# Two-layer hybrid step on one core: output halves weighted before the norm's factor is known, three-pass channel transform, two PSUM groups for the first mLSTM heads, three VectorE passes moved

## The chip, the cores and the metric

One core of one Trainium2 chip runs the whole program in one launch. The metric is device microseconds of one execution. Before the change it is 2081.56 us, the median of 3 runs (2080.41 to 2082.77). Engines are named as in the profile: PE (TensorE matmul), PEld (TensorE weight load), DVE (VectorE), ACT (ScalarE), POOL (GpSimd), SP (SyncE, which issues most DMAs).

## The reference, cut to what matters

1152 tokens (128 of context, 1024 latent) of width 1024 pass two layers. In both, `h = rms_norm(x, g_pre) * (1 + scale) + shift`, a mixer makes `y`, and

```python
x = x + gate * rms_norm(y, g_post)       # rms_norm(y, g) = y * rsqrt(mean(y*y) + EPS) * g
```

Layer 0 has two mixers side by side. The RG-LRU mixer (8 blocks of 128 channels) projects, convolves, gates and scans. The Fourier mixer (8 blocks of 128 channels) computes, for each block,

```python
fr = jnp.fft.fft2(xg, axes=(1, 3), norm='ortho').real        # over tokens and the block's 128 channels
yb = jnp.einsum('blgi,gij->blgj', fr, w_four) + b_four
y  = concat([ya * silu(za), yb * silu(zb)]) @ w_out
```

Layer 1 is a chunkwise mLSTM with 8 heads in both directions: for each head q, k, v, o, z are projected, input and forget gates of all heads come from 32 more columns (`log_sigmoid` of the forget gate, running sums and running maxima over tokens), and 9 chunks of 128 tokens are stepped through.

## The kernel before, in words

**Precision and tiling.** A weight matrix or activation that goes through a large product is split into a high part, rounded to a single-pass format (fp32r, written by ACT), and the rest (`raw - hi`, subtracted by DVE). A product is then three matmul passes: hi x hi, hi x rest, rest x hi. Projections are 8 slices of the contraction times 3 passes times 3 column groups of 384 tokens, 72 matmuls into one PSUM group of three banks (`project`, L126). `PS` holds two groups of three banks, `PX` two more banks. Some small products are single passes on plain fp32; the profile shows two records for each.

**Staging of weights.** `w_load` (SP), `w_split_hi` (ACT, L107) and `w_split_lo` (DVE, L111) bring every 128-column weight tile through two slots. A tile is loaded when its slot's rest has been taken, split high when the product that used the slot has ended, and PE waits for the rest (`w_lo`).

**Order.** Each engine runs a list written out by hand, stage by stage, and waits on semaphores; nothing is reordered at run time. The stages are setup, RG-LRU blocks, Fourier blocks, output product of layer 0 with the next layer's norm, mLSTM heads, output product of layer 1.

**Setup (L420-543).** x is normed, turned and modulated into `h` in 8 slices. ACT writes the even slices' modulated rows and all high parts (L164, L442), DVE the odd slices' modulated rows (L516) and the rests (`h_rows`, L521). DVE takes the rest of the first weight tile inside `h_rows(0)`, between the odd slice's rows and the first slice's rest. The first RG-LRU steps follow: DVE clears the padded input (L816), then computes a softplus (L551 on), and ACT waits for both.

**Fourier blocks (L902-1171).** In block i PE multiplies the channel DFT with `w_four` (L981), projects xb (L126, group 0), in blocks 2 to 5 also sums a part of the remaining modulation (L1011), does the token transform of block i-1 (L997, L1000), then turns xb of block i against the channel weights (`to_tokens`, L987: 9 token tiles, 128x128 against 128x256, 6 into group 0 and 3 into `PX`), and projects zb (L126, group 1). ACT copies xb out of PSUM (L1061) and the 256 channel-weight columns (L1058), both as fp32. On DVE, `outputs(i-1)` (L1137, L1138) waits for the token transform; its end (`y_ready`) lets PE start the zb projection.

**Output product (L1173-1497).** 18 half tiles of 128 tokens x 512 columns, first the left halves, then the right halves, into three banks in turn. When the right half of tile t is done, ACT sums its squares (L1357, written to the scratch `OUTB`) and takes the root (L1361); DVE inverts it (L1427), multiplies both halves by the inverse and the gain rows (L1429, L1431), and adds the residual to the right half (L1435), while POOL adds it to the left half (L1288). In layer 0, ACT then norms x again, PE turns it to channels (L1299), and DVE modulates it in PSUM (L1447) and takes the rest of `h` (L1452). At the end PE computes the gate columns and the first q tile by column groups (L144).

**mLSTM heads (L1551-2230).** `body(j, ...)` projects head j's 8 tiles ("jobs" 0 to 7: q, k, two v tiles, o, z, o, z; job n of head j is written (j, n) below) and steps head j-1's chunks between them. `body(0)` has only jobs 0 to 3. All jobs use PSUM group 0, and PE starts a job when the one before has been copied out by ACT (`pe.wait_ge(evacuated, before(j, n))`); group 1 and `PX` hold the head's chunk work. In `body(0)` DVE works through `forget_gates`: rows of 40 x 1152 elements through a logarithm (`log1p`: a reciprocal, then a series), sums and maxima, with the rests of weight tiles 2 to 5 (jobs (0,2), (0,3), (1,0), (1,1)) put between by a hook. ACT then takes four exponentials (L1944-1947), PE turns them to token order (`gates_to_tokens`, L1743, into group 1), DVE copies them out (`token_scalars`, L2021), PE turns k (L1762) and forms the scores (L1764), DVE weighs k (L2048), and then takes the rest of the next v tile.

## Time and profile before

| | |
|---|---|
| median of the runs | 2081.56 us |
| the profiled execution's own time | 2082.77 us |
| its span, first to last instruction | 2081.2 us, 28432 instructions |
| busy: PE, PEld | 2022.2 us (97%), 1891.3 us (91%) |
| busy: DVE, ACT, POOL | 1049.6 us (50%), 651.8 us (31%), 129.6 us (6%) |
| granted TensorE clock, mean | 0.994 of full speed |

Shares are of the span. The page's second part cuts the span into 40 slices; PE shows nine tenths or more in all but three of them, at the start, in the sixteenth slice (780 to 832 us) and at the end. A row of the trace names an engine, a line of the kernel, the operation, what is written and read, and, in square brackets, how long the engine stood idle just before and what ended that. "x72" is a count of instructions merged into one row.

### The profile page before, as it was taken

What the parts mean: (1) busy time and instruction counts of PE and PEld (TensorE: products, weight loads), DVE (VectorE), ACT (ScalarE), POOL (GpSimd) and SP (SyncE); (2) the same over time, 40 slices, a digit from 0 to 9 for tenths busy, and PEclk for the clock granted to TensorE, in tenths of its full rate; (3) what the DMA queues carried; (4) which work ended last, traced back from release to release, by engine and by line L of the source; (5) the groups of instructions that cost most, each with busy time, mean ns of one, the idle gap of its engine ahead of it and who ended that gap; (6) DMA issues with size and microseconds to landing.
All of it is one profiled execution on the core that took longest, in us unless ns stands there. A gap on an engine that the chain in (4) does not pass through costs nothing.

```text
span 2081.2 us, 28432 instructions
## 1 busy us (share of the span) xinstructions
PE 2022.2 (97%) x11770; PEld 1891.3 (91%) x11770; DVE 1049.6 (50%) x1632; ACT 651.8 (31%) x831; POOL 129.6 (6%) x117
## 2 busy tenths in 40 slices
PE   6999999999999998999999999999999999999998
PEld 5999999999988888989999999999999999998886
DVE  5778885535353574763434334343343433545344
ACT  6677773222234453121212112121121111214422
POOL 0032232000200010000000000000000000000001
PEclk9999999999999999999999999999999999999999
DMA  8221214442246443131221312213122121416554
GB/s 296 66 67 43 73 58 120 142 169 82 70 153 186 153 157 113 35 113 41 82 59 38 102 41 82 59 41 99 41 81 59 46 95 41 101 58 193 174 167 136
DMA packets 218344, 204.59 MB, mean 98 GB/s; under 512 B 13346, under 2 KB 187002, under 8 KB 218098
## 3 DMA queue, kind: packets, MB, share of 16 engines
q1 hardware_dynamic: 214194, 190.52, 30.3%
q0 software_dynamic: 3872, 12.35, 1.7%
q8 instruction: 87, 1.43, 0.3%
q14 instruction: 31, 0.25, 0.0%
q10 hardware_dynamic: 160, 0.05, 0.0%
HBM read 172.14 MB, written 30.59 MB: 97 GB/s over the span
## 4 chain that ended last, share of the span: by engine, by line
PE 80%; issue 8%; POOL 3%; DVE 3%; ACT 3%; DMA 2%; ACTq 0%; POOLq 0%; SPq 0%; DVEq 0%
PE psum_groups L126 37%; PE psum_groups L1207 18%; PE psum_groups L1823 10%; PE psum_groups L1804 3%; PE psum_extra L1795 3%; PE psum_groups L1806 2%; POOL tanh_then_state L635 2%; DMA w_raw<-in_w_in_e 1%; PE psum_groups L997 1%; POOL mixed_y L640 1%; PE psum_groups L144 1%; PE psum_groups L987 1%; PE psum_extra L1011 1%; PE psum_groups L1764 1%; PE psum_groups L1775 1%
## 5 line engine op out<-in xcount | busy, mean ns | idle before, releaser
L126 PE MATMUL psum_groups<-h_hi,w_hi 128*128 128x384 f32 x1896 | 449.5, 345 | 11.4 <-ACT q_t L1916 4.2
L126 PE MATMUL psum_groups<-h_lo,w_hi 128*128 128x384 f32 x1896 | 434.3, 337 | 0.0
L126 PE MATMUL psum_groups<-h_hi,w_lo 128*128 128x384 f32 x1896 | 434.1, 337 | 0.0
L126 PEld LDWEIGHTS psum_groups<-h_hi,w_hi 128*128 128x128 f32 x1896 | 339.1, 188 | 23.0 <-issue 12.6
L126 PEld LDWEIGHTS psum_groups<-h_lo,w_hi 128*128 128x128 f32 x1896 | 340.3, 188 | 0.0
L126 PEld LDWEIGHTS psum_groups<-h_hi,w_lo 128*128 128x128 f32 x1896 | 340.1, 188 | 0.0
L1207 PE MATMUL psum_groups<-w_out,y_tile_hi 128*128 128x512 f32 x1008 | 317.6, 394 | 0.0
L1207 PEld LDWEIGHTS psum_groups<-w_out,y_tile_hi 128*128 128x128 f32 x1008 | 189.6, 188 | 42.6
L2089 DVE SCALAR_TENSOR_TENSOR state<-state,head_decay,psum_extra 128x257 f32<-128x257 f32 x112 | 54.1, 483 | 287.6 <-PE psum_groups L1806 285.5
L1207 PE MATMUL psum_groups<-w_out,y_tile_lo 128*128 128x512 f32 x504 | 198.1, 393 | 0.0
L1823 PE MATMUL psum_groups<-w_hi,h_hi 128*128 128x256 f32 x576 | 165.1, 287 | 4.9 <-DVE w_lo L111 2.1
L111 DVE TENSOR_TENSOR w_lo<-w_raw,w_hi 128x1024 fp32r<-128x1024 f32 x97 | 133.8, 1379 | 68.9 <-ACT w_hi L107 60.9
L1823 PE MATMUL psum_groups<-w_lo,h_hi 128*128 128x256 f32 x576 | 163.1, 283 | 0.0
L1823 PE MATMUL psum_groups<-w_hi,h_lo 128*128 128x256 f32 x576 | 163.1, 283 | 0.0
L107 ACT ACTIVATE w_hi<-w_raw 128x1024 fp32r<-128x1024 f32 x97 | 102.5, 1056 | 70.6 <-PE psum_groups L1823 37.6
L1823 PEld LDWEIGHTS psum_groups<-w_hi,h_hi 128*128 128x128 f32 x576 | 109.3, 190 | 7.0 <-ACT v_rows L1920 3.2
L1207 PEld LDWEIGHTS psum_groups<-w_out,y_tile_lo 128*128 128x128 f32 x504 | 94.8, 188 | 20.8
L1823 PEld LDWEIGHTS psum_groups<-w_lo,h_hi 128*128 128x128 f32 x576 | 109.5, 190 | 0.0
L1823 PEld LDWEIGHTS psum_groups<-w_hi,h_lo 128*128 128x128 f32 x576 | 109.4, 190 | 0.0
L1288 POOL TENSOR_TENSOR x_rows_residual<-out_first_half,x_rows_residual 128x512 f32<-128x512 f32 x18 | 23.3, 1294 | 1356.8 <-DVE out_first_half L1429 1356.8
L273 DVE TENSOR_TENSOR y_tile_lo<-y_tile_raw,y_tile_hi 128x512 fp32r<-128x512 f32 x126 | 80.0, 684 | 35.7 <-ACT y_tile_hi L269 35.2
L1926 ACT ACTIVATE o_tanh<-psum_groups 128x1152 f32<-128x1152 f32 x16 | 18.1, 1132 | 252.6 <-PE psum_groups L126 252.6
(316 smaller groups left out, 2485.7 us busy)
## 6 DMA issues: line engine op xcount, KB each, us to landing
w_raw<-in_w_in_o SPq DMA_DIRECT2D x65, 512.0 KB, 5.2
y_tile_raw<-y_scratch SPq DMA_DIRECT2D x126, 256.0 KB, 3.0
w_raw<-in_w_in_e SPq DMA_DIRECT2D x32, 512.0 KB, 4.0
w_mod_rest<-in_w_mod SPq DMA_DIRECT2D x4, 4096.0 KB, 14.8
y_scratch<-mixed_y POOLq DMA_DIRECT2D x16, 576.0 KB, 3.5
decay_matrix<-gate_rows SPq DMA_DIRECT2D x8, 1152.0 KB, 7.4
q_carry<-gate_rows SPq DMA_DIRECT2D x8, 1152.0 KB, 6.4
y_scratch<-out_gate SPq DMA_DIRECT2D x8, 1152.0 KB, 5.2
```

Source lines behind the costliest of these rows:

```text
L107: act.activation(WHI[:, slot, :], WRAW[:, slot, :], ACT.Copy).then_inc(w_hi, 1)
L111: dve.tensor_tensor(WLO[:, slot, :], WRAW[:, slot, :], WHI[:, slot, :].bitcast(F32), ALU.subtract).then_inc(w_lo, 1)
L126: ins = pe.matmul(PS[:, group, j, 0:JW], w[:, slot, k * P:(k + 1) * P], h(k0 + k)[:, j * JW:(j + 1) * JW], start=start and k == 0 and m == ...
L273: eng.tensor_tensor(y_lo_at(l, n, c), y_raw_at(l, n, c), y_hi_at(l, n, c).bitcast(F32), ALU.subtract).then_inc(yo_lo, 1)
L635: pool.tensor_tensor(both, both, HT[:, 1, p0:p0 + t1 - t0], ALU.add).then_inc(summed, 1)
L1207: ins = pe.matmul(bank(n), y, w[part], start=k == 0 and m == 0, stop=k == 2 * KC - 1 and m == 2)
L1288: pool.tensor_tensor(XR[:, t % 2, 0:DH], out_half(t), XR[:, t % 2, 0:DH], ALU.add).then_inc(x_pool, 1)
L1795: ins = pe.matmul(KV[d][:, 0:DV1], KW[:, d, t * P:(t + 1) * P], V[q][:, t, :], start=True, stop=True)
L1804: ins = pe.matmul(NUM[d][:, 0:DV1], DM[q][:, d, cols], V[q][:, t, :], start=True, stop=s == 0)
L1806: ins = pe.matmul(NUM[d][:, 0:DV1], QW[:, d, cols], C[:, d, :], start=False, stop=True)
L1823: ins = pe.matmul(dst, h[:, k, t * P:(t + 1) * P], w[:, slot, cols], start=k == 0 and m == 0 and n % 2 == 0, stop=k == KC - 1 and m == 2, ...
L2089: ins = dve.scalar_tensor_tensor(C[:, d, :], C[:, d, :], DC[:, d, tiles[d]:tiles[d] + 1], KV[d][:, 0:DV1], ALU.mult, ALU.add)
```

## The change

It has five parts.

1. *Output halves.* DVE multiplies both halves by the gain rows as soon as they are there, the right one after the squares are summed, and then, with the inverse root, does `half * inverse + residual` for both halves. POOL's addition is gone. ACT writes its squares to a PSUM bank, not to `OUTB`.
2. *Channel transform.* In Fourier blocks 1 to 7 `to_tokens` is three single-pass matmuls a tile (27, not 9 fp32 products). ACT writes xb and the channel weights rounded; DVE takes both rests (`operands_rest`), 256 and 1152 columns from PSUM, ahead of `outputs(i-1)`. PE waits for them.
3. *First heads.* Jobs (0,1), (0,3) and (1,1) write PSUM group 1; jobs (0,1) to (1,1) wait for the job before the last. `gates_to_tokens` uses group 0 and waits for (1,0)'s copy, and after it PE waits for (1,1)'s.
4. *DVE passes moved.* The first weight tile's rest goes ahead of `h_rows(0)`; the clearing of the padded input goes into setup; in `forget_gates` the rest of tile (1,0) goes one instruction later in the series; in `body(1)` the rest of tile (1,2) goes from behind `weigh_k` to ahead of it.
5. The buffers get new names and places for it.

```diff
             modulation_vectors(0)
+            w_split_lo(dve, 0, 0)
             for k in range(HALF):
-                h_rows(k, (lambda: w_split_lo(dve, 0, 0)) if k == 0 else None)
+                h_rows(k)
             w_split_lo(dve, 0, 1)
+            dve.memset(XA[:], 0.0).then_inc(pads, 1)
             modulation_vectors(1)
...
+        ch.link(dve.scalar_tensor_tensor(E, E, 1.0, S, ALU.add, ALU.mult))
         if between:
-            between("summed")
-        ch.link(dve.scalar_tensor_tensor(E, E, 1.0, S, ALU.add, ALU.mult))
+            between("series_ready")
...
-            def to_tokens(first, last, bank, done):
+            def to_tokens(i, first, last, bank, done):
+                passes = ((XB, CW), (XBL, CW), (XB, CWL)) if i else ((XB0, CW0),)
                 for t in range(first, last):
-                    ins = pe.matmul(bank(t - first), XB[:, t * P:(t + 1) * P], CW[:].rearrange("p a n -> p (a n)"),
-                                    start=True, stop=True, skip_group_check=True)
+                    for m, (x, w) in enumerate(passes):
+                        ins = pe.matmul(bank(t - first), x[:, t * P:(t + 1) * P], w[:].rearrange("p a n -> p (a n)"),
+                                        start=m == 0, stop=m == len(passes) - 1, skip_group_check=True)
...
             def modulation(i, q):
-                pe.wait_ge(cw_out, i + 1)
+                pe.wait_ge(operands_lo, 2 * i - 1)
...
-                pe.wait_ge(xb_out, i + 1)
-                pe.wait_ge(cw_out, m * 2 + slot + 1)
+                if i:
+                    pe.wait_ge(operands_lo, 2 * i)
...
+            def operands_rest(i):
+                dve.wait_ge(cw_out, i + 1)
+                dve.tensor_tensor(CWL[:].rearrange("p a n -> p (a n)"), PX[:, 1, 256:512],
+                                  CW[:].rearrange("p a n -> p (a n)").bitcast(F32), ALU.subtract).then_inc(operands_lo, 1)
+                dve.wait_ge(xb_out, i + 1)
+                dve.tensor_tensor(by_bank(XBL[:]), PS[:, 0, :, 0:JW], by_bank(XB[:]).bitcast(F32), ALU.subtract
+                                  ).then_inc(operands_lo, 1)
...
                     w_split_lo(dve, i + KC, 1)
+                    operands_rest(i)
                     outputs(i - 1, isinstance(i, int) and i == 1)
...
-                pool.tensor_tensor(XR[:, t % 2, 0:DH], out_half(t), XR[:, t % 2, 0:DH], ALU.add).then_inc(x_pool, 1)
...
-                act.wait_ge(*((half_out, NT * (l + 1)) if t == 0 else (x_ready, NT + t) if l else (x_turned, t)))
-                act.activation(OUTB[:], bank(NT + t), ACT.Square, accum_out=SSB[:, t:t + 1]).then_inc(square_sum, 1)
+                act.activation(PS[:, 1, 2, :], bank(NT + t), ACT.Square, accum_out=SSB[:, t:t + 1]).then_inc(square_sum, 1)
...
+                dve.wait_ge(half_out, NT * l + t + 1)
+                dve.tensor_tensor(out_half(t), out_half(t), g[:, 0:DH], ALU.mult).then_inc(scaled, 1)
+                dve.wait_ge(square_sum, NT * l + t + 1)
+                dve.wait_ge(*((half_out, NT * (l + 1)) if t == 0 else (x_ready, NT + t) if l else (x_turned, t)))
+                dve.tensor_tensor(OUTB[:], bank(NT + t), g[:, DH:D], ALU.mult).then_inc(scaled, 1)
                 dve.wait_ge(y_std, NT * l + t + 1)
                 dve.reciprocal(YSTD[:, t:t + 1], YSTD[:, t:t + 1]).then_inc(y_rstd, 1)
-                dve.wait_ge(y_rstd, NT * l + t + 1)
-                dve.scalar_tensor_tensor(out_half(t), out_half(t), YSTD[:, t:t + 1], g[:, 0:DH],
-                                         ALU.mult, ALU.mult).then_inc(scaled, 1)
-                dve.scalar_tensor_tensor(OUTB[:], bank(NT + t), YSTD[:, t:t + 1], g[:, DH:D],
-                                         ALU.mult, ALU.mult).then_inc(scaled, 1)
...
-                dve.tensor_tensor(x[:, DH:D], OUTB[:], x[:, DH:D], ALU.add).then_inc(x_ready, 1)
+                dve.wait_ge(y_rstd, NT * l + t + 1)
+                for half, done in ((out_half(t), x_pool), (OUTB[:], x_ready)):
+                    cols = x[:, 0:DH] if done is x_pool else x[:, DH:D]
+                    dve.scalar_tensor_tensor(cols, half, YSTD[:, t:t + 1], cols, ALU.mult, ALU.add).then_inc(done, 1)
...
+        FIRST_JOBS = {(0, 1): 1, (0, 2): 0, (0, 3): 1, (1, 0): 0, (1, 1): 1}
+        def group_free(eng, j, n):
+            if isinstance(j, int) and (j, n) == (0, 1):
+                eng.wait_ge(rows_sb, 1)
+            elif isinstance(j, int) and (j, n) in FIRST_JOBS:
+                eng.wait_ge(evacuated, before(j, n) - 1)
+            else:
+                eng.wait_ge(evacuated, before(j, n))
...
                 pe.wait_ge(exps_ready, 4)
+                pe.wait_ge(evacuated, before(1, 1))
                 for n, rows in enumerate((A, E, WK)):
                     for c in range(NT):
-                        ins = pe.transpose(PS[:, 1, n, c * ROWS_N:(c + 1) * ROWS_N], rows[:, c * P:(c + 1) * P],
+                        ins = pe.transpose(PS[:, 0, n, c * ROWS_N:(c + 1) * ROWS_N], rows[:, c * P:(c + 1) * P],
                                            IDENT[0:ROWS_N, 0:ROWS_N])
                 pe.wait_ge(tok_ready, 1)
+                pe.wait_ge(evacuated, before(1, 2))
...
                         token_scalars()
+                        split(2)
                     weigh_k(h, post)
-                    split(2)
-                    if not post:
+                    if post:
+                        split(2)
+                    else:
                         exponents(h, q)
```

## Rows read from the trace of the kernel before

**Rows 1.** Groups by line: operation, count | busy us, mean ns | idle before.
```profile
L1823 PE MATMUL psum_groups<-w_hi,h_hi 128*128 128x256 f32 x576 | 165.1, 287 | 4.9 <-DVE w_lo L111 2.1 <-ACT v_rows L1920 1.5 <-ACT k_t L1918 1.2
L1823 PEld LDWEIGHTS psum_groups<-w_lo,h_hi 128*128 128x128 f32 x576 | 109.5, 190 | 0.0
L273 DVE TENSOR_TENSOR y_tile_lo<-y_tile_raw,y_tile_hi 128x512 fp32r<-128x512 f32 x126 | 80.0, 684 | 35.7 <-ACT y_tile_hi L269 35.2
L1435 DVE TENSOR_TENSOR x_rows_residual<-out_second_half,x_rows_residual 128x512 f32<-128x512 f32 x18 | 21.7, 1205 | 2.2 <-DVE out_second_half L1431 0.5
```

**Rows 2.** Setup in order of time: start us, length us, engine, line.
```profile
33.41 2.34 ACT L442 ACTIVATE h_hi<-norm_tmp 128x1152 fp32r<-128x1152 f32 x2
...
34.47 1.22 DVE L111 TENSOR_TENSOR w_lo<-w_raw,w_hi 128x1024 fp32r<-128x1024 f32 x1
...
35.60 2.62 DVE L521 TENSOR_TENSOR h_lo<-norm_tmp,h_hi 128x1152 fp32r<-128x1152 f32 x2
...
37.10 1.30 PE L126 MATMUL psum_groups<-h_hi,w_hi 128*128 128x384 f32 x3 [1.47 <-DVE h_lo L521]
...
47.37 0.17 DVE L498 TENSOR_TENSOR mod<-psum_extra,channel_vectors 128x8 f32<-128x8 f32 x1 [3.53 <-PE psum_extra L383]
...
59.54 0.17 DVE L551 TENSOR_SCALAR lru_softplus<-lru_softplus 128x16 f32<-128x16 f32 x1 [0.61 <-ACT lru_softplus L728]
```

**Rows 3.** The chain that ended last, Fourier blocks: start us, length us, what.
```profile
338.36 26.79 DMA w_raw<-in_w_in_e
...
534.22 2.59 PE psum_groups L987 x12
```

**Rows 4.** Fourier blocks 1 and 6 in order of time.
```profile
368.53 0.68 PE L981 MATMUL psum_extra<-w_four,channel_dft 128*128 128x128 f32 x4 [2.26 <-ACT token_major L1075]
...
530.24 1.13 ACT L1061 ACTIVATE xb<-psum_groups 128x1152 f32<-128x1152 f32 x1 [9.57 <-PE psum_groups L126]
...
534.53 2.07 DVE L1138 SCALAR_TENSOR_TENSOR mixed_y<-psum_groups,b_four,z_silu 128x1024 f32<-128x1024 f32 x1
```

**Rows 5.** The chain that ended last, end of layer 0 and first heads.
```profile
791.10 6.81 DMA w_raw<-in_w_in_o
...
830.52 1.14 ACT q_t L1916
...
844.68 1.14 ACT k_t L1918
...
845.86 17.37 PE psum_groups L1823 x144
...
901.57 1.81 PE psum_groups L1743 x27
...
908.48 1.14 DVE w_lo L111
...
909.76 18.83 PE psum_groups L1823 x144
```

**Rows 6.** DVE, and for one row ACT, in the first heads.
```profile
851.82 1.23 DVE L111 TENSOR_TENSOR w_lo<-w_raw,w_hi 128x1024 fp32r<-128x1024 f32 x1
...
870.55 1.23 DVE L111 TENSOR_TENSOR w_lo<-w_raw,w_hi 128x1024 fp32r<-128x1024 f32 x1 [4.39 <-ACT w_hi L107]
...
898.88 0.19 ACT L1947 ACTIVATE chunk_decay<-chunk_decay 40x9 f32<-40x9 f32 x1
...
915.45 1.23 DVE L111 TENSOR_TENSOR w_lo<-w_raw,w_hi 128x1024 fp32r<-128x1024 f32 x1 [0.18 <-DVE decay_matrix L2034]
```

**Rows 7.** A stretch: length, busy PE, PEld, DVE, ACT, POOL, granted clock, DMA share, GB/s.
```profile
909.70:912.00 2.30, 2.24 (x14) 2.27 (x15) 2.23 (x2) 0.00 (x0) 0.00 (x0) 0.70 0.00 0
```

**Rows 8.** DVE at the end of the program.
```profile
2073.86 0.17 DVE L1427 RECIPROCAL rows_ystd<-rows_ystd 128x1 f32<-128x1 f32 x1 [8.20 <-ACT rows_ystd L1361]
...
2075.58 1.19 DVE L1435 TENSOR_TENSOR x_rows_residual<-out_second_half,x_rows_residual 128x512 f32<-128x512 f32 x1
```

More of the change, by code:

```diff
@@ L508, in modulation_vectors, with h_rows @@
                 dve.wait_ge(mod_ready, half + 1)
-            def h_rows(k, between=None):
+            def h_rows(k):
                 if k % 2 == 0:
@@ L1057, in group @@
                     act.wait_ge(ub_done, i)
-                act.activation(CW[:].rearrange("p a n -> p (a n)"), PX[:, 1, 256:512], ACT.Copy).then_inc(cw_out, 1)
+                act.activation((CW0 if first else CW)[:].rearrange("p a n -> p (a n)"), PX[:, 1, 256:512], ACT.Copy).then_inc(cw_out, 1)
                 if not first:
@@ L1284, in on_gpsimd @@
         def on_gpsimd(pool):
-            for t in range(NT):
-                pool.wait_ge(mod_then_residual_in[t % 2], 16 * (3 + (NT + 1 - t % 2) // 2 * l + t // 2))
-                pool.wait_ge(scaled, 2 * (NT * l + t) + 1)
-                pool.tensor_tensor(XR[:, t % 2, 0:DH], out_half(t), XR[:, t % 2, 0:DH], ALU.add).then_inc(x_pool, 1)
+            pass
         def on_tensor(pe):
@@ L1837, in job @@
                         return
-                    if not isinstance(j, int) or j or n:
-                        pe.wait_ge(evacuated, before(j, n))
+                    group_free(pe, j, n)
                     if n == 2:
```

49 lines of the change are left out of this document (29 added, 20 removed).

## The prediction

> **What bounds the kernel now.** I read the page first: PE is busy for nearly the whole span, so time can only come out of two places, cheaper PE work and stretches in which PE waits. The chain of waits says where these are, the groups by line give prices by shape, and the timeline of each engine gives the slack beside each wait. Four stretches are touched. In setup PE waits 1.47 us for the first rest of h, and DVE reaches that rest late because a 1.22 us weight pass stands in front of it [rows 2]. In a Fourier block the channel transform is PE work on the chain: 12 records, two for each of 6 tiles, in 2.59 us [rows 3]. At the first mLSTM heads the chain leaves PE for an ACT copy after each job (1.14 us after q, 1.14 us after k) and for a DVE weight pass before the first v product of head 1 [rows 5]. At the very end only DVE, ACT and the last store are left [rows 8].
>
> **The channel transform.** Before, one record takes 2.59 / 12 = 0.216 us, and a block has 18, so 3.89 us. After, it has 27 single passes of 128x128 against 128x256. The v product has this very shape, with a load for each matmul: 144 in 17.37 us [rows 5], 0.1206 us each, so 27 x 0.1206 = 3.26 us and 0.63 us saved a block. Two covers must hold. First, PE now waits for xb's rest. In block 6 ACT's copy ends at 530.24 + 1.13 = 531.37 [rows 4]; the rest, 1152 columns at the price of the 1024-column pass (1.22 us [rows 2], so 1.37), ends near 532.8, and PE wants it at 534.22 [rows 3], behind the token transform: 1.4 us to spare, and more in blocks 2 to 5, where the modulation stands in between too. Should the pass from PSUM cost twice as much, the gain is gone. Second, the zb projection waits for `outputs(i-1)`, which ends at 534.53 + 2.07 = 536.6 [rows 4]; the transform will end at 534.22 + 3.26 = 537.5, still later by 0.9. The small rest (256 columns) is taken 8 us before anybody needs it. Block 1 saves nothing: its successor waits 2.26 us for ACT, which stands behind a weight tile that takes 26.79 us to land [rows 3, 4]; PE will only wait 2.9 us. If that longer pause lets the clock fall it costs up to 1.5 us (the size seen in head 1, below). So 6 x 0.63 = **-3.8 us**, between -4.4 (all seven) and 0.
>
> A rule speaks against this step. Row: loads of 190 ns alternate with matmuls that follow each other every 120.6 ns [rows 1, 5], so here a load costs nothing beyond its matmul. The Trainium skill, "TensorE: Matmul & The Clock Gate", section "Part 3: Packing small matmuls — row/col tiling", says that a weight load runs beside a matmul in flight only when the two use different row groups; these use all rows, so by it each of the 27 passes would show its load. The trace disagrees; what it would make of the time is the slow rival below.
>
> **Setup.** With the weight pass ahead of `h_rows(0)`, DVE does it while it waits for ACT anyway. The first rest can then start when ACT's first high part is there, 33.41 + 2.34/2 = 34.58, not at 35.60 [rows 2]: **-1.0 us**. All later slices follow from it, and PE starts as much earlier; the bounds are 0 (were a modulation weight the real limit) and -1.2 (the whole pass). The clearing of the padded input gives nothing where it stood, since DVE waits 0.61 us more for ACT behind it, and costs nothing where it goes, into a 3.53 us wait [rows 2].
>
> **Output halves.** A tile costs DVE, from the inverse to the end of the last addition, 2075.58 + 1.19 - 2073.86 = 2.91 us [rows 8]. The addition takes 1205 ns while POOL's addition runs beside it; the same shape without POOL takes 684 [rows 1]. After: two products at 0.68, the inverse and two multiply-adds, which with their gaps took 2075.58 - 2073.86 = 1.72, so 3.1 us. Where DVE is the limit, as at the last tile of layer 0, this is +0.1 to +0.2; I take **+0.1** (bounds -0.3 and +0.4, at one place). There the arrival of a weight tile after 6.81 us [rows 5] sets when DVE gets to the tile, and the change moves no transfer ahead of it. At the very end the first product is done early and the second runs beside ACT's root: at most 0.68 and at least 0 of it shows, and I take 0.35. So 0.35 + 1.72 + 0 replaces 2.91, **-0.8 us** (bounds -0.5 and -1.2). In the other tiles PE does not wait for this.
>
> **First heads.** With two groups, (0,1) starts at 830.52, when q's copy starts, not when it ends; a 72-matmul job takes 844.68 - (830.52 + 1.14) = 13.0 us, so it ends at 843.5 [rows 5]. The first v product starts there. Its second half, 8.7 us in, needs a weight rest that DVE finishes at 851.82 + 1.23 = 853.05, behind a reciprocal that nothing moves [rows 6]: PE waits 0.85 us and ends at 861.8. The short v product (8.7), (1,0) and (1,1) (13.0 each) follow without a copy between, to 896.5; before, PE was there at 901.57 [rows 5]: -5.1. This needs the gate chain to be earlier too. Before, DVE waited 4.39 us for a high part that waits for PE's short v product [rows 6]. That product now comes 3 us sooner, and one series step is done before the wait, so I expect the 4.4 us gone, and the last exponential at 899.07 - 4.4 = 894.7, 1.8 us before PE asks.
>
> From the token transposes to the next v product took 909.76 - 901.57 = 8.2 us [rows 5]. Now the weight pass comes before `weigh_k`, and PE needs only the first round of that: transposes 1.81, copies 1.0, weight pass 1.22, head scalars 0.2, two passes of 0.68 and a last score tile, with gaps 6.0 us. Another -2.2 (bounds 0 and -3.3), so -7.3 so far and the v product starts at 902.5. Its second half needs the rest that ended at 916.7 [rows 6]; that pass moves up by 5.1 and by the weight pass that left its front, to some 911.1, and is wanted at 911.2. There is no slack there, and each 0.1 us late costs 0.1. Last, this product took 18.83 us against 17.37 for the one before [rows 5], at a granted clock of 0.70 in its first 2.3 us [rows 7], that is partly at 1.2 GHz, behind a pause in which PE did 3 us of short transposes and then waited 2.1 us. The pause of 2.1 us goes, and I take its -1.5 back (bounds 0 and -1.5). Sum **-8.8 us**, between -3 and -9.5.
>
> **Sum.** -3.8 - 1.0 + 0.1 - 0.8 - 8.8 = -14.3. The profiled execution took 2082.77 us, its span and 1.6 us around it, so 2068.5. The median of the runs shown is 1.2 us lower, 2081.56, and gives 2067.3, which I forecast. Its own range is 2065 to 2070.
>
> **Rivals.** (a) *The gate chain keeps its place.* If what delays it is the DMA and DVE work before the series and not the 4.39 us wait, the last exponential stays at 899.07, PE waits 2.6 us for it, and the longer pause keeps the clock's 1.5 us. For it: every step of the chain is DVE work in order. Against: that wait is plainly for PE. Sum -10.2, 2071.4. (b) *The rest of xb is late.* PE waits for it in every block and the transform's gain is gone: -10.5, 2071.1. For it: only 1.4 us of cover in two blocks. Against: DVE is idle then. (c) *The change does not do what it says:* jobs wait as before because the weight rests become the wait, and three passes cost what two records did. What is left is setup and the end, -1.8, 2079.8. For it: two weight rests in head 0 and 1 already come out within 1 us of need. (d) *The loads show.* With 27 loads of 190 ns in series to their matmuls a block takes 27 x (0.1206 + 0.190) = 8.39 us, 4.5 more than now, in six blocks 27 us, and 2.2 in block 1 beyond its 2.26 us wait: 29.2 - 10.5 = +18.7, 2100. It comes out slower than before as soon as a pass shows more than 90 ns of its load ((10.5/6 + 0.63)/27). Against: 1728 matmuls of this shape, three passes of 576, that don't show it [rows 1].
>
> **Chances.** Forecast 0.57, (a) 0.24, (b) 0.10, (c) 0.06, (d) 0.03. Differences under 0.2%, 4.2 us, can't be told from no change here. Faster takes the forecast, (a), (b) and a little of (c): 0.92. Within 0.2%: most of (c), 0.05. Slower: (d), 0.03. The range takes the forecast's own with (a) and (b): down to 2064 (all bounds on the fast side give -4.4 - 1.2 - 0.3 - 1.2 - 9.5 = -16.6, and the runs shown lie up to 1.2 us under their median) and up to 2073.5 (rival (a) with block 1's 1.5 us of clock, rounded up).
>
> **What would show it.** The records of `to_tokens` 0.12 us apart and 3.3 us for a block; the zb projection 3.3 us behind the token transform; an idle entry for PE behind `operands_rest` would show (b), one above 2.3 us in block 1 its lost share. PE's first projection near 36.1 us. In head 0 no PE wait for ACT's copies, one of some 0.9 us for a weight rest inside the first v product, and none for the exponentials; a wait there is (a). Full granted clock in head 1's first v product. From the last inverse to the last store's issue 2 us, not 2.9. The prediction is wrong if PE's waits in heads 0 and 1 stay above 4 us in sum, or if the matmuls of the transform stand 0.2 us apart.

## The result, and the profile after

The changed kernel takes 2063.41 us (median of 4 runs, 2061.91 to 2064.62) against 2082.16 for the kernel before (4 runs, 2080.41 to 2084.25): ratio 0.9908, 95% interval 0.9896 to 0.9921, so 16.4 to 21.7 us less. The forecast was 2067.3 in a range from 2064.0 to 2073.5. The direction was right, the gain was a third larger, and the time lies 0.6 us under the range. A second series gave 0.9916 (0.9902 to 0.9931).

The profiled execution after took 2062.97 us, its span 2061.4, 19.8 us shorter than before. The chain that ended last, in the Fourier blocks and in the first heads (start us, length us, what):

```profile
336.93 27.45 DMA w_raw<-in_w_in_e
...
368.44 14.07 PE psum_groups L126 x72
...
390.33 2.15 PE psum_groups L995 x18
392.47 1.08 PE psum_extra L995 x9
...
831.13 1.38 DMA row_m<-in_state_mlstm_m
...
845.40 1.24 DVE w_lo L111
...
846.68 17.36 PE psum_groups L1856 x144
864.04 25.35 PE psum_groups L126 x144
889.39 1.82 PE psum_groups L1775 x27
...
895.63 17.33 PE psum_groups L1856 x144
```

The channel transform, 12 records and 2.59 us for six tiles in [rows 3], is 18 records in 2.15 us, and 27 in 3.23 with the last three tiles. In the heads no ACT copy stands on the chain any more: two jobs follow each other in 25.35 us, and the token transposes start at 889.39 where [rows 5] had 901.57. The late tile ahead of block 2 is still there, 27.45 us for 26.79, and the 72 projections behind it take 14.07 us, where before they took 12.49:

```profile
369.21 12.49 PE psum_groups L126 x72
```

The end, in order of time (start us, length us, engine, line):

```profile
2056.05 0.69 DVE L1445 TENSOR_TENSOR out_second_half<-psum_groups,gain_rows_latent 128x512 f32<-128x512 f32 x1 [8.23 <-ACT psum_groups L1372]
2056.05 0.29 ACT L1376 ACTIVATE rows_ystd<-rows_ssb,rows_ssa 128x1 f32<-128x1 f32 x1
2056.65 0.15 DVE L1447 RECIPROCAL rows_ystd<-rows_ystd 128x1 f32<-128x1 f32 x1
2056.94 0.75 DVE L1453 SCALAR_TENSOR_TENSOR x_rows_residual<-out_first_half,rows_ystd,x_rows_residual 128x512 f32<-128x512 f32 x1
2057.61 0.74 DVE L1453 SCALAR_TENSOR_TENSOR x_rows_residual<-out_second_half,rows_ystd,x_rows_residual 128x512 f32<-128x512 f32 x1
2058.43 0.34 SPq L1263 DMA_DIRECT2D y_sample<-x_rows_residual  x1
```

The second product runs beside ACT's root, as forecast, and from the start of the inverse to the last sum's end it is now 1.70 us, before 2.91 [rows 8].

Where the 19.8 us of the two traces lie (checkpoints on PE, before against after):

```
stretch                                       forecast   the two traces
setup, to the end of the recurrent half          -1.0        -1.4
Fourier blocks 2 to 7, six transforms            -3.8        -3.95
block 1: tile later 0.6, projections slower 1.6   0          +2.15
output halves of layer 0                         +0.1        -1.85  (0.7 at tile 0, 1.15 at a weight tile)
first heads                                      -8.8       -10.55
later heads, untouched                            0          -0.2
last head, untouched, behind its pause            0          -1.65
end, to the last store's issue                   -0.8        -0.9
end, behind the store's issue                     0          -1.4
```

Three lines were to be explained: a gain in the output halves and behind the last store where almost nothing was expected, more in the heads, and differences where nothing was changed.

### The profile page after: what moved, and what is told of

Same layout as the page of the kernel before. It is cut to its first block, busy times and chain, and to the rows that moved or that the text cites. A ratio compares the mean times of both kernels' runs of the same rounds, so it can differ in the third digit from the quotient of the medians.

```text
span 2061.4 us, 28554 instructions
## 1 busy us (share of the span) xinstructions
PE 2012.9 (98%) x11833; PEld 1886.2 (92%) x11833; DVE 1062.7 (52%) x1664; ACT 651.7 (32%) x831; POOL 106.1 (5%) x99
## 4 chain that ended last, share of the span: by engine, by line
PE 79%; issue 9%; POOL 3%; DVE 3%; ACT 3%; DMA 2%; SPq 0%; ACTq 0%; POOLq 0%; DVEq 0%
PE psum_groups L126 36%; PE psum_groups L1226 19%; PE psum_groups L1856 10%; PE psum_groups L1837 3%; PE psum_extra L1828 3%; PE psum_groups L1839 2%; POOL tanh_then_state L638 2%; DMA w_raw<-in_w_in_e 1%; PE psum_groups L1005 1%; POOL mixed_y L643 1%; PE psum_groups L144 1%; PE psum_extra L1019 1%; PE psum_groups L1797 1%; PE psum_groups L995 1%; PE psum_groups L1808 1%
## 5 line engine op out<-in xcount | busy, mean ns | idle before, releaser
L1837 PE MATMUL psum_groups<-v_rows,decay_matrix 128*128 128x257 f32 x288 | 84.8, 380 | 0.0
```

The source lines that it names most:

```text
L1837: ins = pe.matmul(NUM[d][:, 0:DV1], DM[q][:, d, cols], V[q][:, t, :], start=True, stop=s == 0)
```

## Experiments

Each result is given as the ratio to the kernel before of the same series.

**The four parts alone.** Each kernel is the one before with one part of the change. Their cores:

```diff
  only_setup
+            w_split_lo(dve, 0, 0)
             for k in range(HALF):
...
  only_transform
+                passes = ((XB, CW), (XBL, CW), (XB, CWL)) if i else ((XB0, CW0),)
...
  only_outputs
-                pool.tensor_tensor(XR[:, t % 2, 0:DH], out_half(t), XR[:, t % 2, 0:DH], ALU.add).then_inc(x_pool, 1)
...
  only_heads
+        FIRST_JOBS = {(0, 1): 1, (0, 2): 0, (0, 3): 1, (1, 0): 0, (1, 1): 1}
...
```

> Kernel before with the setup edits alone (weight rest ahead of the first rows of h, clearing of the padded input moved). Theory of terms (each part gives what the prediction's sum gave it): -1.0 us, first projection of the recurrent half on PE near 66.4 us instead of 67.4. Reading of the two traces: -1.45 us, 66.0. Nothing behind it is touched, so it is also a second look at the untouched stretches: if the gain of 1.9 us at the last head (18.8 us from the pause to the end of its first projections) and the 1.4 us at the last store are chance, they may turn up here too; if they are the work of one of the other parts, the last head stands as in the kernel before, with a projection of 6.6 us behind the pause and a last store that lands over 4 us after its issue.

> Kernel before with the three-pass channel transform in Fourier blocks 1 to 7 alone. Theory of terms: -3.8 us, 3.25 us a block instead of 3.89 in blocks 2 to 7, nothing in block 1. Rival, the clock: the longer pause that block 1 now leaves PE in (2.9 us instead of 2.3) lets the granted clock fall, and the 72 projections behind it take 14.1 us instead of 12.5, in which case -2.3 us is left. If the slow projection behind block 1 in the changed kernel was chance, they take 12.5 here.

> Kernel before with the output halves weighted ahead of the norm alone (no GpSimd addition). Theory of terms: -0.7 us: +0.1 at the first tile of the attention output, -0.8 at the very end. Rival from the two traces: -2.8 to -4.2 us, because PE's wait before the first output tile (0.7 us) goes, the stores of the rows of x leave about 1.1 us earlier and with them the weight tile that PE of the gates waits for, and the last store lands 1.4 us sooner without a GpSimd sum in front of it. If those are scatter of the transfers, the checkpoints at 711.5 and 806.7 us stay within 0.5 us of the kernel before.

> Kernel before with the two PSUM groups for the first heads and the moved vector passes of these heads alone. Theory of terms: -8.8 us between the start of the q job and the first step of the later heads. Reading of the two traces: -10.5 us, of which 1.3 is a gate chain whose small transfers land sooner and the rest a v product of head 1 at full clock. Rival: the 1.3 us belong to the output halves, which free the queues or GpSimd ahead of the gates; then it is -9.3 or less here and shows under the output halves.

```
part              ratio (95%)                us by it   forecast
only_setup        0.9993 (0.9984 to 1.0003)    -1.5       -1.0
only_transform    0.9982 (0.9973 to 0.9991)    -3.8       -3.8
only_outputs      0.9975 (0.9966 to 0.9984)    -5.2       -0.7
only_heads        0.9940 (0.9926 to 0.9953)   -12.5       -8.8
```

So the output halves are the part that was forecast most wrongly, and the interval of the heads (-9.8 to -15.4) leaves the forecast out as well; setup and transform agree. The sum, -23.0, is more than the whole change gave; with half-widths of 2 to 3 us each that says nothing of an interaction. All four ratios are also taken against the same 26 executions of the kernel before (median 2083.94 us, where the other series have 2080.54 to 2083.86), so an error of theirs enters the sum four times.

The trace of setup alone does not show its gain by itself: the projections of the recurrent half start at 67.40 us, 67.43 before, where I had expected 66.0 to 66.4. Over all profiles without idle PE work at the start (see the end of this section) they start at 67.4 to 68.3 us in five with the old setup and at 66.0 to 68.4 in nine with the new; the means are 68.0 and 66.9, so 1.1 us of gain under a scatter of over 2.

The traces show where the output halves gain. From the first matmul of the output product to the turn of its first tile it is 120.14 us in all six profiles with the old code there and 119.49 in all eleven with the new: PE had waited 0.65 us, a wait that I had overlooked. ACT, before and with the output halves alone, in order of time:

```profile
702.60 1.28 ACT L1361 ACT_TABLE_LOAD   x1
...
707.36 1.03 ACT L1368 ACTIVATE psum_extra<-x_rows_residual 128x1024 f32<-128x1024 f32 x1 [2.12 <-DVE x_rows_residual L1435]
```

```profile
706.46 1.03 ACT L1364 ACTIVATE psum_extra<-x_rows_residual 128x1024 f32<-128x1024 f32 x1 [0.79 <-DVE x_rows_residual L1434]
```

At tile 0 ACT loads a table (1.28 us) ahead of the root, so both products are done by then, and DVE's chain behind the root is 1.3 us shorter; PE waited for it. The weight tile that gained 1.15 us in the pair gained 0.4 here. From the turn of tile 0 to the first product of the gates it is 88.5 to 90.6 us in the six profiles with the old code (mean 89.9) and 88.3 to 90.2 in the eleven with the new (mean 89.3): most of the 1.15 was transfer scatter, and whether the 0.7 between the means is the change's is open. The other gain is at the end, below.

In the heads alone PE waits 1.5 us for the weight rest behind the reciprocal, and in the changed kernel not at all:

```profile
PE psum_groups L1838 <- DVE w_lo L111: 1.5, 1, 1.5
```

With that wait, and with a stretch of half the clock behind the token transposes, this trace has 7.9 us of gain between the gates' products and the later heads, where the changed kernel has 10.5; the 12.5 timed is not found in it. The gate chain starts when the last of its small loads lands (the gates' biases and a row of the old state, called biases below): from the issue of the last one to the first addition it took 2.8 us before, 1.9 with the heads alone, 1.5 in the changed kernel, and 1.5 with the transform alone, where nothing near it differs. I took that for scatter; more on it below. A half-rate stretch is one in which the granted clock is 0.5, 1.2 GHz instead of 2.4. That of the last head (1801 us before) is missing with setup alone, though nothing is edited within 1700 us of it.

**The changed kernel again**, and **each half of the heads' edit undone**:

> The changed kernel once more, for a second profile and a closer ratio. The four parts alone were -0.5, -3.5, -5.1 and -11.6 us by their medians. If they add up: -20.6 us against the kernel before. Theory of chance for the surprises in the first pair of traces: the half-rate stretches of the TensorE clock fall on other pauses than last time, the transfer of the biases lands 1.4 to 3.3 us after its issue, and the last head's projection behind its pause may take 6.3 or 8 us; the end (last inverse to the end of the span 4.8 us) and the missing pauses in heads 0 and 1 must come back exactly. Rival, that the change causes them: full clock in the last head and in head 1's first v product, and the biases landing within 1.5 us, once more.

```diff
  no_groups: the hunks of the two groups left out
-                        dst = PS[:, group_of(j, 2 if first == 0 else 3), n // 2, n % 2 * DV:(n % 2 + 1) * DV]
+                        dst = PS[:, 0, n // 2, n % 2 * DV:(n % 2 + 1) * DV]
...
  no_moves: the passes back in the old order
...
-                        split(2)
                     weigh_k(h, post)
-                    if post:
-                        split(2)
-                    else:
+                    split(2)
+                    if not post:
...
```

> The changed kernel with the first heads back on one PSUM group; the moved vector passes stay. Theory of terms: the copies after q, k, v, q and k come back onto the chain, 1.14 us each, and the 5.1 us up to the token transposes are lost, so +5.1 us against the changed kernel, some +4 to +6; the 2.2 us between the transposes and the next v product stay. Rival: the gain up to the transposes came from the gate chain and the moved passes, not from the groups; then under +2 us.

> The changed kernel with the vector passes of the first heads back in their old order (the weight rests behind the series step and behind the weighing of k); the two PSUM groups stay. Theory of terms: 2.2 us between the token transposes and the next v product are lost, and up to 1.5 of clock with the pause that comes back; the groups' 5.1 us stay unless the weight pass of the series now waits again for the short v product. So +2.2 to +3.7 us against the changed kernel. Rival: PE finds the weight rest in time either way; then nothing.

The changed kernel gave 0.9916 and a span of 2062.4. The end and the missing pauses came again; so did the full clock in the last head and the early biases, which speaks against chance for these two; but head 1's first v product was no longer at full clock. The granted clock from the token transposes on, first trace, then second (stretch: length, busy PE, PEld, DVE, ACT, POOL, granted clock, DMA share, GB/s):

```profile
892.20:895.60 3.40, 3.33 (x29) 3.25 (x30) 3.22 (x5) 0.00 (x0) 0.00 (x0) 1.00 0.81 316
```

```profile
892.20:895.60 3.40, 3.40 (x20) 3.40 (x20) 3.30 (x6) 0.00 (x0) 0.00 (x0) 0.60 0.68 271
```

Same code, same pause of 1.08 us ahead of it: 1.00 in one, 0.60 in the other, and the v product 1.2 us later. Over the 17 profiles taken here, those of the experiments below among them:

```
pause                                            profiles with 1.2 GHz behind it
ahead of block 0's token transform, 2.0 us          10 of 17
last head, 1.9 us, the same code in all             10 of 17
head 1's first v product, order of before            4 of 5
the same, changed heads                              6 of 12
end of Fourier block 1, three passes                 7 of 8
end of Fourier block 1, one product                  2 of 7
```

(Two kernels that change the end of block 1 otherwise, `early_tokens` and `mod_later` below, are left out of its lines.) So the last head's 1.65 us is chance: unchanged code goes either way. Head 1 has the slow stretch less often than before, but still in half of the profiles.

With one group the ratio is 0.9936, 4.2 us behind the changed kernel (forecast +5.1; each of the two intervals reaches about 3 us to either side), and the copies are back on the chain:

```profile
825.03 1.14 ACT q_t L1934
826.21 12.96 PE psum_groups L126 x72
839.20 1.14 ACT k_t L1936
840.38 17.37 PE psum_groups L1841 x144
857.77 1.46 ACT v_rows L1938
...
881.96 1.14 ACT q_t L1934
883.14 12.94 PE psum_groups L126 x72
896.08 1.81 PE psum_groups L1761 x27
```

The transposes stand 6.7 us later than at 889.39 in the changed kernel, and 7.1 from the gates' products on, where this run was 0.4 us ahead. A 72-matmul job that a copy follows shows 12.96 us, two back to back 25.35, 12.68 each: the end of one job runs beside the start of the next, 0.3 us at every handover that goes.

With the old order of the passes the ratio is 0.9923, +1.5 us by it, inside the scatter. In the traces 8.98 us lie between transposes and v product, 7.48 in the second trace of the changed kernel, both with a half-rate stretch: 1.5 us for the forecast's 2.2.

**GpSimd at the end.**

```diff
         def on_gpsimd(pool):
-            pass
+            if l:
+                pool.wait_ge(y_rstd, NT * (l + 1))
+                pool.tensor_tensor(GAINC[0][:, 0:DH], GAINC[1][:, 0:DH], GAINC[1][:, DH:D], ALU.add).then_inc(pool_tail, 1)
```

> The changed kernel with one idle addition of 128x512 on GpSimd behind the last inverse, whose sum nobody reads (it overwrites gain rows that are no longer used). The last store of the kernel before lands 2.1 us before the end of the span, that of the changed kernel 0.75 us. Theory: the program ends when GpSimd has drained, about 4.8 us after its last addition, and the addition that the change removed held the end back by 1.4 us. Then the tail is longer here again: the addition ends near 1.3 us behind the inverse, the span 5 us behind that, 1.5 us more than in the changed kernel. Rival: the store itself landed sooner, for the addition's sake or by chance; then the end stays 0.75 us behind the landing.

Its one execution has a span of 2062.8 us. The kernel before, and then this one:

```profile
2074.96 1.26 POOL L1288 TENSOR_TENSOR x_rows_residual<-out_first_half,x_rows_residual 128x512 f32<-128x512 f32 x1 [9.84 <-DVE out_first_half L1429]
...
2076.84 0.34 SPq L1244 DMA_DIRECT2D y_sample<-x_rows_residual  x1
```

```profile
2056.48 1.85 DVE L1456 SCALAR_TENSOR_TENSOR x_rows_residual<-out_first_half,rows_ystd,x_rows_residual 128x512 f32<-128x512 f32 x1
2056.53 1.26 POOL L1307 TENSOR_TENSOR gain_rows_context<-gain_rows_context 128x512 f32<-128x512 f32 x1 [1161.50 <-DVE rows_ystd L1450]
2058.25 0.74 DVE L1456 SCALAR_TENSOR_TENSOR x_rows_residual<-out_second_half,rows_ystd,x_rows_residual 128x512 f32<-128x512 f32 x1
2059.06 0.34 SPq L1264 DMA_DIRECT2D y_sample<-x_rows_residual  x1
```

From the start of GpSimd's last addition to the end of the span it is 2081.2 - 2074.96 = 6.24 us before and 2062.77 - 2056.53 = 6.24 us here; 6.25 in each of the three parts that keep the addition. The trace holds the reason in a record that no view lists: a DRAIN of GpSimd that starts with the last addition and takes 6.04 us, from 2074.93 to 2080.97 before and from 2056.50 to 2062.53 here. In the changed kernel it lies at 899.61, long over, and the last DRAIN is SyncE's, at 2061.20, behind the store. The last store lands 2.1 us ahead of the end before and 1.5 here, but 0.75 in the changed kernel, where GpSimd has long been idle. The theory holds. From the start of the inverse to the end it is 6.58 us against 4.77, 1.8 more where I expected 1.5: 0.7 of it stands behind the landing, and 1.1 is the store itself, which left later because DVE's pass beside GpSimd took 1.85 us instead of 0.75.

**Block 1.** Two ways to take its pause back, and the kernel before once more:

```diff
  early_tokens: ScalarE takes the next tile's high part behind the token rows
-                    if i < KC - 1:
+                    if 1 < i < KC - 1:
                         w_split_hi(act, i + KC + 1, 0)
...
+                if i == 1:
+                    w_split_hi(act, i + KC + 1, 0)
                 projected(act, i + KC, 1)
...
  block1_two: block 1 as before
-                passes = ((XB, CW), (XBL, CW), (XB, CWL)) if i else ((XB0, CW0),)
+                passes = ((XB, CW), (XBL, CW), (XB, CWL)) if i > 1 else ((XB0, CW0),)
...
```

> The changed kernel with one step of ScalarE moved in Fourier block 1: the token rows of the transform are copied out before the high part of the next weight tile is taken, not behind it. In the changed kernel that copy stands idle behind a tile that lands near 364.4 us, the rows come out at 367.6, PE waits 2.0 to 2.6 us and the clock halves behind the pause in every profile with three passes. Theory (block 1's end is this queue on ScalarE): PE starts block 2's projection on the tile's rest alone, near 366.8 instead of 368.4, so -1.6 us, and the pause shrinks to some 1.2 us; if the pause is what costs the clock, another -1.6. Rival (the tile's landing alone sets block 2): the projection starts as late as before, nothing gained.

> The changed kernel with block 1's channel transform as one product of full-width operands, as in the kernel before; blocks 2 to 7 keep three passes. Theory of terms: block 1's three passes saved nothing, because PE waits there anyway, so the block ends at the same time, the pause is 0.65 us shorter, and if the longer pause is what halves the clock behind it (6 of 6 profiles with three passes, 1 of 4 without), the 72 projections of block 2 take 12.5 us again instead of 14.1: -1.6 us against the changed kernel. Rival: the clock falls at this place by chance; then the same, within what a run scatters.

> The kernel before once more, for a second profile. Theory of chance: the half-rate stretches fall on other pauses than in the first (there behind 342, 805, 908 and 1799 us), the biases of the gates land 1.4 to 3.3 us after their issue. Steady, if they are the kernel's: the span ends 2.1 us behind the landing of the last store, 2.9 us lie from the last inverse to the store's issue, and PE pauses behind each of the first heads' jobs for 0.9 us or more.

Ratios 0.9904 (0.9887 to 0.9920) and 0.9901 (0.9885 to 0.9918): the same as the changed kernel within the scatter; the gains expected, 1.6 to 3.2 us and 1.6, are no larger than these intervals. The trace of the first, the chain:

```profile
338.57 27.75 DMA w_raw<-in_w_in_e
...
366.34 1.07 ACT w_hi L107
...
367.44 1.24 DVE w_lo L111
...
368.81 12.75 PE psum_groups L126 x72
```

From the tile's landing to the projection 2.5 us, in the changed kernel 4.1: the 1.6 us of the queue on ScalarE, as expected, and the projection runs at full clock. With block 1 in one product it takes 12.49 us too. But in both traces a half-rate stretch stands one pause earlier, at 353.8 and 355.2 us, behind PE's wait ahead of block 1's own zb projection. With one product in block 1:

```profile
354.38 14.33 PE psum_groups L126 x72
...
369.15 12.49 PE psum_groups L126 x72
```

So neither trace shows that the shorter pause kept the clock; the cost had been paid one pause ahead. Of the 17 profiles 16 have a half-rate stretch that starts between 340 and 375 us, one or two of them, behind one of the pauses there. The theory that the longer pause costs the clock rests on the counts in the table alone, 7 of 8 against 2 of 7.

The kernel before again has a span of 2079.3, and, between setup and the end, half-rate stretches behind block 0 and the last head only. Both of its pauses at 806 and 908 us are there, at full clock. Steady are the jobs' copies and the end, 6.2 us behind GpSimd's addition.

**What makes the tile late.**

```diff
-            w_mod_columns(0)
             for i in range(1, KC - 1):
                 for slot in range(2):
                     w_load(sp, i + KC + 1, slot, in_tile(a["w_in_e"][0], i * P + P + (2 + slot) * D))
+                if i == 1:
+                    w_mod_columns(0)
```

> The changed kernel with one load moved on SyncE's queue: the 4 MB of modulation weights (w_mod_rest, issued at 336.5 us, landed at 360.1, first needed near 382) are issued behind block 2's two weight tiles instead of ahead of them. Theory: this load is what makes the tile land 27.4 us after its issue and the last rows of y 13.2 us after theirs, and these two cause PE's pauses in block 1 (2.6 us at 350, 2.0 to 2.6 at 366, the clock's 1.6 us behind the second). Then the tile lands within 6 us, both pauses go, the three passes of block 1 save their 0.65 us like the others, and block 2's projection starts near 363.5 instead of 368.4: -4.6 us, -6.2 with the clock, against the changed kernel. Rival (the load only moves its delay): the next tiles, the small channel weights that are issued at 355 and needed near 361, now stand beside it and land after 362, and no more than the first pause, 2.6 us, is gained, or nothing.

Ratio 0.9878 (0.9860 to 0.9896), median 2058.18 us: 6 to 8 us ahead of the changed kernel by the two ratios of that, and the fastest kernel here. The tile's load in the changed kernel, with the 4 MB ahead of it, and then here (KB, us from issue to landing):

```profile
w_mod_rest<-in_w_mod SPq DMA_DIRECT2D x1, 4096.0 KB, 23.6
w_raw<-in_w_in_e SPq DMA_DIRECT2D x1, 512.0 KB, 27.4
```

```profile
w_raw<-in_w_in_e SPq DMA_DIRECT2D x1, 512.0 KB, 4.5
```

And its chain, where PE goes from block 0 through block 1 into block 2 without a pause:

```profile
349.19 2.26 PE psum_groups L996 x18
351.45 1.08 PE psum_extra L996 x9
352.52 12.48 PE psum_groups L126 x72
365.01 0.45 PE psum_extra L988 x4
365.45 12.49 PE psum_groups L126 x72
```

Block 2 starts at 365.45 instead of 368.44, although the recurrent half ended 1.9 us later in this run: 4.9 us gained (expected 4.6), and 1.6 of clock behind it. It is the one profile of the 17 without a half-rate stretch between 340 and 375 us. The small channel weights landed at 360.8, in time.

**The gate chain.** By now the chain had started late in all five profiles without the three-pass transform (1.9 to 3.6 us behind the last bias's issue) and early in all nine with it (1.3 to 1.6), 300 us behind the transform. That is no scatter. In the first heads a load of 16 KB on an instruction queue goes with every 210 to 300 PE instructions, over the program with 252 in the middle, a matmul and its weight load counted as two, and the transform adds PE instructions. (The Trainium skill, "Runtime: NRT & Kernel Launch", section "Instruction fetch mechanics", gives 256 instructions for such a block and calls its cost mostly hidden; the trace agrees with the first.) The queues beside the bias transfers, 7 us before, and then after (packets, MB, share):

```profile
q1 hardware_dynamic: 1178, 0.61, 36.8%
q8 instruction: 1, 0.02, 0.8%
```

```profile
q1 hardware_dynamic: 1175, 0.60, 38.1%
```

Three kernels move that load by idle transposes on PE at the start and edit nothing else:

```diff
             turn_vectors(0, 96, (vec_in, 16 * 5))
+            for _ in range(62):
+                pe.transpose(PX[0:32, 0, 0:32], VR[0:32, 0, 0:32], IDENT[0:32, 0:32])
```

> The changed kernel with 62 idle 32x32 transposes on PE at the start, in a pause of 4.2 us there; nobody reads them. In 14 profiles so far a load of 16 KB on the queue for instructions starts every 250 to 270 PE instructions. In the five without the three-pass transform it falls between 1.5 us ahead and 0.6 us behind the issue of the last gate bias, and the first addition of the gate chain starts 1.9 to 3.6 us behind that issue; in the nine with it, which have more PE instructions ahead, it falls 10 to 12 us ahead, and the addition starts after 1.3 to 1.6 us. Theory (the load holds the biases up): the 124 instructions added here put the next load within 1 us of the last bias again, and the addition starts 1.9 to 3.6 us behind it; PE then waits up to 1.5 us for the weight rest behind the reciprocal. Rival (the transform speeds the biases in some other way, or it is chance): 1.3 to 1.6 us as in the changed kernel.

> The kernel with the first heads' part alone, with 57 idle 32x32 transposes on PE at the start. It has no three-pass transform; its load of instructions falls 1.5 us ahead of the last bias, the addition starts 1.9 us behind that, one issue on SyncE takes 1.3 us instead of 0.3, and PE waits 1.5 us for the weight rest. Theory: the 114 instructions added put the load some 10 us ahead, the addition starts after 1.3 to 1.6 us, no issue is held up, and the 1.5 us wait of PE goes or shrinks under 0.3. Rival: nothing of that changes.

> The changed kernel with 59 idle transposes at the start instead of 62, so that the load of instructions starts about 0.5 us later than with 62, where it started 0.07 us ahead of the last bias's issue, took 0.93 us, was over 0.1 us before the bias's first packet counted, and the addition started after 1.4 us as in the changed kernel. Theory (what counts is a load still under way when the last bias's packets run, 1.0 to 1.4 us behind the issue): now the load runs from 0.4 to 0.6 us on, as in the four kernels in which the addition started after 2.8 to 3.6 us, and the addition starts after 2.5 us or more. Rival (the place of the load has nothing to do with it): 1.3 to 1.6 us once more.

```
kernel         base, transposes       load against       last bias's issue   PE waits for
                                      last bias's issue  to first addition   the weight rest
only_heads     -                        -1.5 us            1.9 us               1.5 us
fetch_early    only_heads, 57          -10.9 us            1.4 us               0
fetch_late     changed kernel, 62       -0.1 us            1.4 us               0
fetch_later    changed kernel, 59       +0.5 us            1.5 us               0
```

Moving the load away took the delay away: the held-up issue on SyncE (1.3 us) is back at 0.3, and the 1.5 us wait of PE is gone, by nothing but 114 idle instructions 800 us earlier. Putting a load back beside the biases did not bring the delay back, not even where it ran over the same time as in the four slowest cases (from 0.4 to 0.6 us on). So the theory that a load beside the biases delays them falls in that form. Shown is that the place of the instructions in the program moves the gate chain by 1.4 us; what the load does to the biases in some kernels and not in others stays open. It is the 30th load of its queue in the five slow profiles and the 31st in the last two runs, which I could not vary by itself.

## Why the prediction was wrong, point by point

**Channel transform: right.** 3.23 us a block (forecast 3.26), 0.66 saved in each of six (0.63). The rest of xb never stopped PE, so rival (b) is out. 27 passes in 3.23 us are 119.6 ns each with their loads of 190 ns hidden. By the rule of the Trainium skill, "TensorE: Matmul & The Clock Gate", "Part 3: Packing small matmuls — row/col tiling", as the prediction took it, they would show (the same section also lets a load run ahead that targets the background weight buffer); the trace disagrees with the rule, and rival (d) is out. For block 1 the forecast was nothing saved with a risk of up to +1.5 for the clock. The risk came in seven of eight profiles; it belonged into the sum, not into the bounds.

**Setup: right, with some luck in the first pair.** -1.4 by the first two traces, outside the bounds (0 to -1.2), -1.1 by the means of all profiles, -1.5 timed alone (interval -3.3 to +0.6), forecast -1.0.

**Output halves: this is the step that failed.** The prediction put "+0.1" for layer 0 and "In the other tiles PE does not wait for this", and -0.8 for the end. Two terms were missing. At tile 0 PE does wait: -0.65, by the very mechanism that I had worked out for the end. And I followed DVE, ACT and the last store to the end but not GpSimd, whose addition I knew to be removed: -1.4, shown by the added one, with which the span ends 6.24 us behind GpSimd's start again. The -0.9 to the store's issue is within the bounds given (-0.5 to -1.2). At the last tile of layer 0, where I put the +0.1, the stretch from the weight rest to the end of the rest of h took 6.40 us before and 6.37 after: nothing. Together about -3.0 instead of -0.7. Without the two missing terms, 2.05 us, the median would stand near 2065.5 (an estimate from these rows), inside the range. The part timed alone gave -5.2 (-3.3 to -7.1), a little more than these rows account for.

**First heads: mechanism right, terms mis-sized.** Up to the token transposes the forecast was -5.1 and the traces show -7.1, twice in the changed kernel; without the groups 7.1 come back. Two sizes were off: each new job was charged with 13.0 us read from its start to the copy behind it, where jobs back to back take 12.68, some 0.9 us on three jobs; and the 0.85 us wait for the weight rest fell to nothing, because the biases came 1.3 us earlier, an effect of the transform's instructions on the program's layout that no reading of the code near the heads could give (in the heads alone the wait is 1.5 us). The exponentials ended at 888.31, 5.7 us earlier than the start of the heads explains (forecast 4.4) and 1.1 us before PE asked, so rival (a) is out. Between transposes and v product 1.95 us were saved in the first trace (8.19 to 6.24), 2.2 forecast. The rest for the second half of that product was ready at 904.01, 0.3 us ahead of need, where the forecast saw no slack; it moved up 0.5 us more than the transposes, though the weight pass that the prediction says had left its front still stands there. The 1.5 us of clock were in the first trace; but six of twelve profiles with changed heads still have a half-rate stretch there, against four of five with the old order, so by these counts some 0.5 us of this credit was due. That the first trace had all of it was luck. Rival (c) is out with the copies.

**Untouched stretches.** 1.65 at the last head is scatter of the clock, and most of the 1.15 at a weight tile that of transfers. They flatter the first pair, whose difference in span (19.8) lies above both timed ones (19.2 and 17.5 by their ratios).

Adding what the traces bear out: setup -1.1, transform -3.95 with about +0.9 for block 1's clock (1.58 us, in 7 of 8 profiles instead of 2 of 7), outputs -3.0, heads -9.05 without clock (7.1 and 1.95), together -16.2, against 17.5 timed (14.4 to 20.4) and 19.2 (16.4 to 21.7). What is left, 1.3 to 3.0 us, is explained only in part, by the 0.5 of clock in the heads and perhaps by the 0.7 at the weight tile.

## What to carry to other kernels

Follow every engine to the end of the program: one that finished its part early can still hold the end, and an operation removed there is worth its tail as well. Read a job's length from two that follow each other, not from one that waits for its reader. Where a tile lands late, look at what the same queue issued just ahead of it: moving one 4 MB load behind two tiles gave 6 to 8 us, about what the transform and the output halves gave together (7.0 by the traces, 9.0 timed alone).

## What the hardware did that I had not expected

The span ended 6.24 to 6.25 us after the start of GpSimd's last 128x512 addition in seven profiles of six kernels, while the addition itself is shown with 1.26 us; GpSimd's DRAIN record, 6.03 to 6.04 us in all seven, covers the rest. (The Trainium skill, "Perfetto Trace Analysis", section "GPSIMD Engine Instruction", says that a GpSimd span in a profile is not to be relied on; no run here shows whether the 1.26 us are right.) A DVE multiply-add of 128x512 took 1.85 us beside it and 0.75 alone. Behind a pause of 1.1 to 2.1 us, in unchanged code, the clock fell to 1.2 GHz in about half of the profiles; where it was measured it cost 1.2 to 1.9 us, as much as a small part of this change. And 114 idle PE instructions at the start moved small transfers 800 us later by 1.4 us.
